# A two-layer hybrid trunk on one core: level differences moved from GpSimd to VectorE, slots of the feed-forward stage shifted by one

## The reference, cut to what matters

```python
for i in range(DEPTH):
    mod = c_act @ ada_w[i] + ada_b[i]
    sh1, sc1, g1, sh2, sc2, g2 = jnp.split(mod[:, None, :], 6, axis=-1)
    h = rms_norm(x, norm_mix[i]) * (1.0 + sc1) + sh1
    y = dilated_attention(h, ...) if i % N_MIXERS == 0 else hgrn2_mixer(h, ...)
    x = x + g1 * y
    h = rms_norm(x, norm_ffn[i]) * (1.0 + sc2) + sh2
    x = x + g2 * swiglu(h, ffn_w1[i], ffn_w3[i], ffn_w2[i])
# in hgrn2_mixer, with G the cumulative log of the gate:
    diff = G[:, :, :, None, :] - G[:, :, None, :, :]
    decay = jnp.exp(jnp.where(tri, diff, -jnp.inf))
    A = jnp.einsum('bhtk,bhsk,bhtsk->bhts', qq, kq, decay)
```

## Time and profile before

| | us |
|---|---|
| median of three runs | 845.66 |
| profiled execution, its own time | 845.91 |
| its span | 843.8 |
| TensorE busy | 822.7 (97%) |
| VectorE busy | 591.5 (70%) |
| ScalarE busy | 437.6 (52%) |
| GpSimd busy | 121.2 (14%) |

### The profile page before, as it was taken

One profiled execution on the slowest core, in us unless ns is written; L12 is line 12 of the kernel. 1 busy time (PEld: TensorE's weight loads), 2 busy tenths in 40 slices (PEclk: granted clock), 3 DMA queues, 4 the chain that ended last, 5 costly groups with the idle time before them and its releaser, 6 DMA issues.

```text
span 843.8 us, 12202 instructions
## 1 busy us (share of the span) xinstructions
PE 822.7 (97%) x4864; PEld 672.4 (80%) x4864; DVE 591.5 (70%) x739; ACT 437.6 (52%) x565; POOL 121.2 (14%) x154
## 2 busy tenths in 40 slices
PE   7999999999999999999999899999999999999998
PEld 3678889888889887888788688878788888887886
DVE  1787797697797786777688676777779756645544
ACT  5376454464455576433344275796786644334421
POOL 3010101111111000111021000466720000000000
PEclk9999999999999999999999999999999999999999
DMA  9998878878877446899798655443444566765521
GB/s 326 367 357 259 283 253 255 271 251 251 273 246 263 151 150 210 270 301 312 244 314 298 230 174 194 136 149 125 150 151 158 193 211 221 262 204 178 172 99 50
DMA packets 122139, 189.06 MB, mean 224 GB/s; under 512 B 5715, under 2 KB 91080, under 8 KB 122084
## 3 DMA queue, kind: packets, MB, share of 16 engines
q1 hardware_dynamic: 109828, 146.10, 53.3%
q0 software_dynamic: 12256, 42.18, 14.5%
HBM read 187.18 MB, written 1.09 MB: 223 GB/s over the span
## 4 chain that ended last, share of the span: by engine, by line
PE 80%; DVE 7%; POOL 4%; issue 3%; ACT 3%; DMA 2%; SPq 1%; POOLq 0%; ACTq 0%; DVEq 0%
PE bank L520 68%; POOL arena L414 3%; PE bank L768 2%; DMA arena<-in_ada_w_dram 2%; PE bank L796 2%; POOL arena L413 2%; PE bank L749 1%; PE bank L913 1%; PE bank L604 1%; PE bank L777 1%; DVE wlo L1477 1%; PE bank L620 1%; DVE wlo L1485 1%; PE bank L641 1%; DVE arena L1622 1%
## 5 line engine op out<-in xcount | busy, mean ns | idle before, releaser
L1477 DVE TENSOR_TENSOR wlo<-raw,whi 128x2048 fp32r<-128x2048 f32 x119 | 273.0, 2299 | 48.1 <-ACT whi L1050 47.9
L1050 ACT ACTIVATE whi<-raw 128x2048 fp32r<-128x2048 f32 (+1 forms) x125 | 235.6, 1888 | 23.1 <-DMA raw<-in_attn_w_qkv_dram 13.9
L520 PE MATMUL bank<-whi,hT_hi 128*128 128x512 f32 (+1 forms) x728 | 196.4, 394 | 3.8 <-issue 2.9
L520 PE MATMUL bank<-wlo,hT_hi 128*128 128x512 f32 (+1 forms) x752 | 195.0, 383 | 0.0
L520 PE MATMUL bank<-whi,hT_lo 128*128 128x512 f32 (+1 forms) x728 | 187.6, 381 | 0.0
L520 PEld LDWEIGHTS bank<-wlo,hT_hi 128*128 128x128 f32 x752 | 138.5, 190 | 28.2
L520 PEld LDWEIGHTS bank<-whi,hT_hi 128*128 128x128 f32 x728 | 129.9, 189 | 33.3 <-issue 10.3
L520 PEld LDWEIGHTS bank<-whi,hT_lo 128*128 128x128 f32 x728 | 133.3, 189 | 26.6
L397 POOL DMA_DIRECT2D ada_w<-in_ada_w_dram x80 | 42.6, 533 | 489.3 <-DVE acc L1498 489.3
L1498 DVE SCALAR_TENSOR_TENSOR acc<-ada_w,cact,acc 128x1024 f32<-128x1024 f32 x80 | 102.3, 1279 | 12.8 <-DMA ada_w<-in_ada_w_dram 11.8
L1317 ACT ACTIVATE arena<-bank 128x256 f32<-128x256 f32 x44 | 14.5, 381 | 163.4 <-PE bank L520 163.4
(11 more groups left out here) (192 smaller groups left out, 789.3 us busy)
## 6 DMA issues: line engine op xcount, KB each, us to landing
raw<-in_ffn_w_dram SPq DMA_DIRECT2D x88, 512.0 KB, 4.9
ada_w<-in_ada_w_dram POOLq DMA_DIRECT2D x80, 512.0 KB, 5.0
raw<-in_attn_w_qkv_dram SPq DMA_DIRECT2D x60, 512.0 KB, 5.9
raw<-in_ffn_w_dram SPq DMA_DIRECT2D x22, 1024.0 KB, 5.0
raw<-in_hgrn_w_in_dram SPq DMA_DIRECT2D x16, 1024.0 KB, 5.3
arena<-in_ada_w_dram SPq DMA_DIRECT2D x16, 512.0 KB, 10.0
raw<-in_attn_w_qkv_dram SPq DMA_DIRECT2D x4, 1024.0 KB, 7.3
raw<-in_attn_w_out_dram SPq DMA_DIRECT2D x4, 1024.0 KB, 6.4
```

What stands on the lines that cost most here:

```text
L520: mm = nc.tensor.matmul(dst[t][c][:, 0:n], lhs[:, k0 + k, t * P:(t + 1) * P], w[:, k, c * 512:c * 512 + n], start=start and k == 0, stop=s ...
L1050: return nc.scalar.activation(dst, src, ACT.Copy)
L1477: nc.vector.tensor_tensor(wlo[:, m % RAW, :], raw[:, m % RAW, :], fp(hi_of(m)), ALU.subtract).then_inc(s["split"], 1)
```

## The change

Four things are done.

1. `rec_diff` goes from GpSimd's list to VectorE's. It stands there behind the scales of the step, one step ahead of the step that uses it. It waits for r_q of the level two before and for a new semaphore r_Z, which says that ScalarE has read the keys' half of the buffer.
2. ScalarE takes the queries' exponential first (r_E), then the keys' (r_Z). TensorE waits for both r_q and r_Z.
3. For half 1, VectorE's `rec_key` is moved ahead of step 7's split, and ScalarE's `rec_log_key` from step 7 to behind step 8's rounding.
4. In the first feed-forward stage the adaLN pieces spread over slots 3 to 28, not 4 to 28, and the task of block 9 is done in slot 24, not 25; so its turn and its taking out are in slot 26, not 27.

```diff
-            def rec_diff(half, level):
-                E, G, Gk = rE[:, level % 2], rG[half], rGk[half]
-                pool.wait_ge(s["r_G"], half + 1)
-                if LEVELS * half + level > 2:
-                    pool.wait_ge(s["r_q"], LEVELS * half + (level - 1) // 2 * 2)
...
-                    pool.tensor_tensor(v(E)[:, :, 0, :], mid, v(Gk)[:, :, 0, :], ALU.subtract)
-                    i = pool.tensor_tensor(v(E)[:, :, 1, :], v(G)[:, :, 1, :], mid, ALU.subtract)
...
@@ rec_product
                     pe.wait_ge(s["r_q"], LEVELS * half + level)
+                    pe.wait_ge(s["r_Z"], LEVELS * half + level)
@@ rec_exp
-                nc.scalar.activation(Z[:, :, 0, :], E[:, :, 0, :], ACT.Exp)
                 nc.scalar.activation(E[:, :, 1, :], E[:, :, 1, :], ACT.Exp).then_inc(s["r_E"], 1)
+                nc.scalar.activation(Z[:, :, 0, :], E[:, :, 0, :], ACT.Exp).then_inc(s["r_Z"], 1)
@@ ScalarE, loop over steps
-                if step in (3, 7):
-                    rec_log_key(step // 7)
+                if step in (3, 8):
+                    rec_log_key(step // 8)
@@ VectorE
+            def rec_diff(half, level):
+                E, G, Gk = rE[:, level % 2], rG[half], rGk[half]
+                dve.wait_ge(s["r_G"], half + 1)
+                if LEVELS * half + level > 2:
+                    dve.wait_ge(s["r_q"], LEVELS * half + level - 2)
+                    dve.wait_ge(s["r_Z"], LEVELS * half + level - 2)
...
+                    nc.vector.tensor_tensor(v(E)[:, :, 0, :], mid, v(Gk)[:, :, 0, :], ALU.subtract)
+                    i = nc.vector.tensor_tensor(v(E)[:, :, 1, :], v(G)[:, :, 1, :], mid, ALU.subtract)
...
@@ VectorE, loop over steps
                 for scale in scales:
                     rec_scale(*scale)
+                for half, o in products_at(step + 1):
+                    if o >= 2:
+                        rec_diff(half, o - 1)
...
                 if step == 9:
                     rec_decay(1)
+                if step == 7:
+                    rec_key(1)
                 if step:
                     split_unit(M_IN + step + AHEAD)
...
-                if step in (3, 7):
-                    rec_key(step // 7)
                 if step == 3:
+                    rec_key(0)
                     rec_decay(0)
@@ tasks_at
-    late = {3: [6], 12: [7], 17: [8], 18: [9], 25: [10]}
+    late = {3: [6], 12: [7], 17: [8], 18: [9], 24: [10]}
@@ ada_in_ffn
-    first, last, n0, n1 = (4, 28, ADA_FFN0, ADA_FFN1) if f == 0 else (3, 18, ADA_FFN1, 2 * ADA_BLOCKS * KC)
+    first, last, n0, n1 = (3, 28, ADA_FFN0, ADA_FFN1) if f == 0 else (3, 18, ADA_FFN1, 2 * ADA_BLOCKS * KC)
```

## The result

The kernel after took 835.96 us (median of four runs, 835.68 to 836.18), beside 845.89 for the kernel before (four runs, 844.59 to 846.48) on the same chip: a ratio of 0.9885, with a 95% interval of 0.9867 to 0.9902. The profiled execution took 836.05, its span is 834.2 where it was 843.8. The forecast was 836.6.

A forecast was written before the change was run, and what follows sets the result against it. TensorE was taken as the bound, busy 97%, gains only from its waits or lower clock. 845.9 less 0.95 (slot 17), 4.7 (slot 28: 3.0 and 1.7) and 3.6 (recurrence), 9.25 in all, gave 836.6 us; range 834.2 to 841.5.

The forecast's parts named there:

- The idle stretch ahead of slot 28 (3.0): TensorE's wait before slot 28, read as one for task 10's copy to mod_b; moving the task saves 3.0 us.
- The lower clock behind it (1.7): Slot 28's first twelve matmuls, partly at 1.2 GHz after the idle stretch; 1.7 us go with that stretch.
- Slot 17 (0.95): TensorE's wait ahead of slot 17 for the sixteenth adaLN piece; the earlier spread saves 0.95 us.
- The recurrence (3.6): With differences on VectorE, most of TensorE's waits in the recurrence go; unit 15 starts at 615.9, gain 3.6 us.
- the bounds of 4.7 and 2.0: Recurrence gain: 4.7 us if no wait stays, 2.0 us if a subtraction costs VectorE 0.69.
- the walk: Each engine's after order in the recurrence laid out on traced durations, each waiting for its semaphores; gives the 3.6 us gain.
- the scale's row: A VectorE scale of 128 x 512, next instruction 0.61 later, result after 0.69; taken as a subtraction's cost.
- the bound of 30.5: Sign of being wrong: steps 11 to 14 of the recurrence taking over 30.5 us.
- Takes "near 1.56 a pair everywhere": Sign on VectorE: without GpSimd beside it every pair of takes is near 1.56 us, against 2.77 beside it.
- rival 3: A subtraction costs VectorE 1.05 us, as on GpSimd alone, so the recurrence loses 7.0: 847.2 us, chance 0.03.
- The key's idle 2.8 in step 7: VectorE idles 2.8 us in step 7 as the moved rec_key waits for ScalarE's gates; said to be hidden.
- steps 8, 9 and 14: Recurrence steps where TensorE should wait for the first scale, by 0.3 to 0.4 us each.

The follow-up runs named there:

- task_only: The kernel before with only block 9's adaLN task done in slot 24, pieces still from slot 4: 841.19 us, ratio 0.995.
- task19: The kernel after with task 9 of the adaLN split in slot 19 instead of 18: 835.34 us, ratio 0.9888.
- rec_only: The kernel after with the slots of the kernel before, so only the recurrence's changes: 841.86 us, ratio 0.9959.
- diffs_alone: The kernel before with only the differences moved to VectorE; keys' exponential first, no r_Z, keys and slots as before: 843.77 us, ratio 0.998.
- slots_only: The kernel before with only the changed slots (pieces from slot 3, block 9's task in slot 24): 840.55 us, ratio 0.9942.
- after_again: The kernel after, unchanged, measured a second time: 837.59 us, ratio 0.9901.
- double_sub: The kernel after with both subtractions of levels 1 to 7 done twice on VectorE: 855.89 us, ratio 1.0106.
- take_both_flat: The kernel after with the takes of levels 1 and 2 written into 64 adjacent columns, so the output differs: 835.52 us, ratio 0.9881.

## Why the prediction was right, and where it was not

**The idle stretch ahead of slot 28 (3.0):** right. The profile had put it down to "issue"; the copy to mod_b 0.1 us ahead of its end was the only evidence, and task_only shows it was enough. The wait ahead of slot 18 is the same case: it is called "issue" too, and the 0.68 us copy of task 8 ends it (task19).

**The lower clock behind it (1.7):** right for the execution that was profiled, wrong as a consequence. Behind the same idle 2.85 us, rec_only and diffs_alone have 1.00. The level is not fixed by the order of the work. That this gain stood whole in the comparison of the two profiles is luck.

**Slot 17 (0.95):** mis-sized. It came (slot 17's reduction starts 0.76 earlier in a trace that runs 0.18 late until then: 405.28 against 405.10), but I did not follow the sums into slots 16 to 18: slot 16's waits for its load, slot 17's is done ahead of the gate's copy (412.41), and slot 18 waits 0.49. Net 0.4 here (0.76 and 0.18 less the 0.54 lost between 406.20 and 413.20), 0.6 between the medians of slots_only and task_only. In before the copy stood at 410.23, ahead of need.

**The recurrence (3.6):** 3.2 measured, inside the bounds of 4.7 and 2.0. The path there was another in step 7: it takes 8.23 (6.94 before and in the walk), and the later steps win all but 0.4 of that 1.3 back, since VectorE's list sets the pace there (39.34 of 40 us busy). Steps 11 to 14 take 30.07 us, where the walk had 30.0; after_again has 30.79 (581.02 to 611.81), so the bound of 30.5 that I set was tighter than one kernel's executions are. The duration carried over: 0.68 long, 0.60 apart, against 0.69 and 0.61 from the scale's row. double_sub shows how near it was: VectorE has 0.7 of 40 us left.

**Takes "near 1.56 a pair everywhere":** wrong. I had put the pair of 2.77 in the earlier trace rows down to GpSimd, from one row. It was level 1's and 2's spacing, GpSimd or not. The walk took 1.56 there, 1.2 too little in steps 7 and 12. The same slip is in rival 3's "every 128 x 512 row is 0.69 or less": takes are 0.72 and more. What GpSimd did cost shows in the splits of before:

```profile
544.18 1.52 POOL L413 TENSOR_TENSOR arena<-arena 128x512 f32<-128x512 f32 x1
545.11 2.75 DVE L1477 TENSOR_TENSOR wlo<-raw,whi 128x2048 fp32r<-128x2048 f32 x1 [3.27 <-ACT whi L1050]
...
580.40 3.49 POOL L413 TENSOR_TENSOR arena<-acc,ada_w 128x512 f32<-128x512 f32 x1 [5.79 <-DVE ada_w L1879]
583.10 2.95 DVE L1477 TENSOR_TENSOR wlo<-raw,whi 128x2048 fp32r<-128x2048 f32 x1
```

They are 2.28 now. A split that starts while GpSimd is at a difference is longer by about what is left of that difference: 0.59 left (to 545.70) and 0.47 longer, 0.79 left (to 583.89) and 0.67 longer. A difference that starts while a split runs takes 3.1 to 3.5 and not 1.0 to 1.1. The Trainium skill, "SBUF — State Buffer", section "Who interferes with whom", has a VectorE instruction with two inputs in SBUF and a GpSimd one that reads SBUF contend for a shared port, and calls that an exclusive lock. For the splits the trace agrees (2.75 and 2.95 against 2.28); for the takes it was the wrong reading.

**The key's idle 2.8 in step 7:** none in after, where the key is at 555.94 and ScalarE's gates are done at 555.83. Two things used the 2.8 up. The long takes had moved VectorE back by 1.2. The other 1.6 is the clock at steps 3 to 5: TensorE reached step 5 6.5 us earlier than in before (532.86, 539.34), VectorE its next split only 4.9 (540.21, 545.11). In after_again that stretch is slow, as in before, and the idle time is there, 1.36. This also moves TensorE's waits. They were forecast at steps 8, 9 and 14, 0.3 to 0.4 each; in after_again they are at steps 8 and 14 (0.25, 0.70), in after at steps 7 and 14 (0.33, 0.38). The other two traces with this recurrence agree: task19 (11.81 from step 3 to step 5) waits 0.29 at step 7, rec_only (12.89) waits there for nothing. No run changes the stretch alone, so this rests on four traces. The walk had the order of the waits right for the slow stretch that it took over from before's trace without saying so. In after the takes forecast too short and the idle time that did not come cancel in part.

**The sum:** 9.25 forecast, 9.9 measured, and 8.0 the second time. By the two profiles' spans it is 9.6, and the parts make 9.95, 0.4 too much (0.2 of it is the late start of after's trace): slots 0.95 + 3.0 - 0.5, the clock behind slot 28 1.7, the recurrence 3.2, and 1.6 at steps 3 to 5 (13.42 before, 11.81 after), which I did not forecast and which is the clock again: in after_again that stretch took 13.38 once more, and that kernel's median was 837.59. So 3.3 of the 9.6 are clock levels that another execution may have otherwise, and about 6.3 are order. The forecast held the first of the two and not the second; that it came this near is in part luck. Of the fourteen traces, five have the short stretch at steps 3 to 5 (11.8) and nine a longer one (12.7 to 13.4), and one kernel (after) has both.

**Open:** the 0.7 "issue" in step 7 (554.98) lies within the second of two products, 114 matmuls into 128, where no semaphore is waited for. It is in after and, at 0.18, at the same matmul in double_sub; take_both_flat has 0.26 called issue in step 7. It is not in task19 or after_again. No run tells what it is.

## What to carry to other kernels

A wait that the profile calls issue can be one for a semaphore (here raised by copies of 0.15 and 0.68 us): look in the code for what is waited for, and in the timeline for an instruction that ends just ahead of it. When work is moved onto an engine, take its duration from a row of the same size and strides on that engine, then walk the list to the end of the stretch, past the place where the wait was: an earlier sum delayed a copy two slots on. A long instruction beside another engine's work is contention only if the same instruction elsewhere, with the same strides, is short. And a walk that starts from one trace takes over how far each engine was behind in it: a slow stretch of TensorE ahead of the stage is slack that the next execution may not have.

## What the runs showed of the hardware

- A take of 128 x 512 (a copy under a mask out of a bank) is 0.72 to 0.77 us long when it writes side by side or in runs of four columns and more. Writing every second column or every second pair adds 0.57 (a pair of takes: 2.76, 2.19 with one of the two side by side, 1.62 with both).
- Behind the same instructions and the same idle time TensorE's granted clock was 1.00 in some executions and 0.50 in others (step 3: 1.00 over 521.6 to 525.0 in after, 0.50 over 523 to 525 in after_again, which are the 2.4 and the 1.2 GHz level; four matmuls take 0.92 or 1.71 us from start to start). Such a stretch cost 1.6 to 1.7 us. The Trainium skill, "TensorE: Matmul & The Clock Gate", section "What's actually happening", says that one kernel has a varying number of slow matmuls at its start. The trace shows the same in a kernel's middle, at 474 and 522 us.
- In after VectorE started instructions of 128 x 512 (two inputs in SBUF) that are 0.68 long every 0.60 us, and was busy 39.34 of 40 us.
- A VectorE split that started during a GpSimd difference was longer by about that difference's rest (less 0.12 us), and a difference that started during a split took 3.1 to 3.5 us in place of 1.0 to 1.1.
